# Layers' attention with the values stationary: two heads in two column halves, results that come out turned

## Chip, cores and metric

One core of one Trainium2 chip. The metric is the time of one execution in device microseconds (us), lower is better. TensorE is called PE here, its weight loads PEld, VectorE DVE, ScalarE ACT, GpSimd POOL, SyncE SP.

## What is computed

The reference is two blocks for one sequence of 256 tokens of width 1024, all in float32. The first block has attention, a gated delta rule and a routed mixture of 32 experts. The second block is two layers, and the change lies in their attention:

```python
for l in range(2):
    h = rms_norm(x, norm_mix[l]); z = h @ w_in[l]
    ...
    y_a = sparse_indexed_attention(qa, ka, va, qi, ki, wi, rel_bias, topk)   # 8 heads of 64
    y_b = latent_attention(qb, kb, vb)                                       # 8 heads, values of 64
    # each: p = softmax(logits); y = einsum('bthk,btkhd->bthd', p, v)
    gate_a = sigmoid(ga + b_gate[:D]); gate_b = sigmoid(gb + b_gate[D:])
    merged = gate_a * (y_a @ w_proj_a[l]) + gate_b * (y_b @ w_proj_b[l])
    x = x + merged @ w_out[l]
    ... # a gated convolutional feed-forward part
```

## The kernel before

Every engine has its own instruction list, and they meet through semaphores. Partition dimension is 128, so the 256 tokens are two token tiles (`tt` or `qt`, 0 and 1). PSUM is eight banks of 128 x 512 float32; `layer_plan` (L102) lists the jobs of a layer in the order in which banks are dealt out, round-robin over the eight. A producer waits for `room` (the bank's last user has read it), signals `full`; a reader waits for `ready`, signals `free`; `taken` is true once it has been read. So the order of names in that list decides which job waits for which. The layer's weights come in 2 MB pieces through four ring slots, loaded by SP; the load of a slot waits until the job that reads the slot's earlier weights is full (`loads2`, with the pair ("pa", 3) for the first projection).

The attention of a layer is four calls, `n` = 0 to 3: part a for token tile 0, part a for tile 1, part b for tile 0, part b for tile 1. A call for tile `qt` has `qt + 1` key tiles. Its steps:

- PE `scores` (L2048, through `scores_t`, L522; matmuls on L534) writes the scores of eight heads to `as` or `bs`. Heads are laid out by place: place p holds head 2(p % 4) + p // 4, that is 0, 2, 4, 6, 1, 3, 5, 7.
- DVE `soften_v` (L470) adds the bias or mask, takes the maximum.
- ACT `exps_s` (L507) writes the exponentials into `expo2[qt]` and their sums into `den[qt]`.
- PE `values_t` (L537) turns the exponentials, block by block of 128 x 128, into `at` or `bt` (L546), ACT `turned_s` (L516) copies each bank of four blocks to `PT2`, and PE multiplies (L554): a turned block (128 keys x 128 queries) is stationary, the head's values (128 keys x 64) move, so the result has the queries on its partitions and all eight heads side by side in one bank, `ao` or `bo`. An fp32 matmul is two instructions in the trace, a turn is one.
- DVE `result_v` (L497, its scaling on L502) divides by the sums and writes `ya` or `yb`, tokens on the partitions.
- PE `features("yaT")` turns `ya` (L576), ACT copies it, and `tokens("pa")` (matmuls on L604) multiplies it with the projection for both token tiles and two halves of 512 columns. The same for b.

PE's order behind the queries and keys is written out by hand (L2086 to L2103):

```python
scores(0) gates_t(1) scores(1) gates_t(2) values(0) scores(2) gates_t(3) values(1)
scores(3) values(2)  features yaT  tokens pa  values(3)  features ybT  tokens pb  turns mT  wo
```

DVE forms the gates (`gates_v`, a reciprocal of 128 x 1024 on L1771) between the calls, then multiplies the `pa` and `pb` banks with them (L1799, L1804) and adds (L1808) into `h`, whose storage is also `expo2[1]`. PE turns `h` (`mT`, L1988), ACT copies it, and `wo` follows (L604). Between the layers and ahead of the feed-forward part, `keep_running` (L581) issues twelve plain bf16 matmuls (L585) into the bank of the first `hT` or `fT`, for which it waits. `dn` are the four banks of the last projection of a layer, which DVE adds to `x` on L1630. The expert part uses half-width matmuls: 64 stationary columns, in column half 0 and column half 1 by turns (L1259, L1240).

Of the kernel before, what the change touches and what calls it, by code (L numbers as in the profile page):

```python
# [18 lines left out]
ALU = mybir.AluOpType  # L19
# [3 lines left out]
P = 128  # L23
T = 256
TT = T // P
D = 1024
# [75 lines left out]
def layer_plan():  # L102
    p = Plan()
    for name, n in (("hT", 4), ("cv", 1), ("qi", 2), ("m1", 2), ("m2", 2), ("kiT", 1), ("ix0", 2), ("ix1", 4),
# [4 lines left out]
                    ("wo", 4), ("fT", 4), ("up", 2 * UPC), ("dn", 4)):  # L109
        p.add(name, n)  # L110
    return p
# [106 lines left out]
def split(ap, n):  # L218
    return ap.rearrange("p (a b) -> p a b", a=n)
# [41 lines left out]
    "an_c", "an_q",  # L261
    "gsig",
    "b_in", "bst", "bn",
    "attn_m", "attn_e",
    "mg",
    "yconv", "fexp", "act",
    "out",
# [3 lines left out]
def build_program(nc, A, consts, out):  # L271
# [4 lines left out]
    with ctx:  # L276
# [45 lines left out]
        def area(at, n):  # L322
            return arena[:, at:at + n]
# [101 lines left out]
        def head(place):  # L425


            return 2 * (place % 4) + place // 4

        def ada_rows_t(pe, g):  # L430

            pe.wait_ge(*B.room(f"ag{g}"))
            rows = B.bank(f"ag{g}")
            for i in range(4):
                j = 4 * g + i
                pe.matmul(rows[32 * i:32 * i + 32, :], ident[0:12, j:j + 1].to_broadcast([12, 32]), badr[0:12, :],
                          start=True, stop=False)
            for a in range(4):
                w, landed = w1_slot(ada_at[g] + a)
                pe.wait_ge(*landed)  # L440
                for k in range(2):
                    for i in range(4):
                        ins = pe.matmul(rows[32 * i:32 * i + 32, :], silu_c[:, 2 * a + k, :],
                                        split(w, 2)[:, k, i * CH:(i + 1) * CH], start=False, stop=(a == 3 and k == 1))
            ins.then_inc(B.full(f"ag{g}"), 1)
# [51 lines left out]
        def result_v(v, then, B, S, jobs, call, dst, den, flag="attn_e"):  # L497
# [6 lines left out]
                            den.rearrange("p (b a) -> p b a", b=2).unsqueeze(3).to_broadcast([P, 2, 4, 64]), ALU.mult)\  # L504
             .then_inc(B.free(jobs[2]), 1)

        def exps_s(act, S, qt, call, scale, buf, amax, den):  # L507

            p4 = split(buf, 8)
            act.wait_ge(S["attn_m"], call + 1)  # L510
            for hd in range(8):
                ins = act.activation(p4[:, hd, :], p4[:, hd, :], ACT.Exp, bias=amax[:, hd:hd + 1], scale=scale,
                                     accum_out=den[:, hd:hd + 1])
            ins.then_inc(S["attn_e"], 1)
# [21 lines left out]

        def values_t(pe, B, S, jobs, qt, call, val, buf, PT, flag="attn_e"):  # L537

            p4 = split(buf, 8)
            pe.wait_ge(S[flag], call + 1)  # L540
            for j in range(2 * (qt + 1)):
                pe.wait_ge(*B.room(jobs[1], j))
                for i in range(4):
                    blk = 4 * j + i
                    hd, kt = blk // (qt + 1), blk % (qt + 1)
                    ins = pe.transpose(B.bank(jobs[1], j)[:, i * P:(i + 1) * P], p4[:, hd, kt * P:(kt + 1) * P], ident)  # L546
                ins.then_inc(B.full(jobs[1], j), 1)
            pe.wait_ge(*B.room(jobs[2]))
            for place in range(8):
                for kt in range(qt + 1):  # L550
                    blk = place * (qt + 1) + kt
                    if blk % 4 == 0:
                        pe.wait_ge(*B.taken(jobs[1], blk // 4))
                    ins = pe.matmul(B.bank(jobs[2])[:, place * 64:(place + 1) * 64], PT[:, blk * P:(blk + 1) * P],  # L554
                                    val(head(place), kt), start=(kt == 0), stop=(kt == qt))
            ins.then_inc(B.full(jobs[2]), 1)

        def mean_squares(act, count):

            for tt in range(TT):  # L560
                ins = act.activation(h[:, tt, :], x[:, tt, :], ACT.Square, accum_out=ss[:, tt:tt + 1])
            ins.then_inc(S["ss"], 1)
# [911 lines left out]
        qbT, kbT = split(extra(0, 2 * D), 8), split(extra(2 * D, 2 * D), 8)  # L1474
        qb, kb = split(extra(4 * D, 1536), TT), split(extra(4 * D + 1536, 1536), TT)
        vb = split(extra(4 * D + 3072, D), TT)
        ya, yb = split(area(4 * D, D), TT), split(area(5 * D, D), TT)
        yaT, ybT = split(area(9728, D), 4), split(area(10752, D), 4)
        expo2 = [area(8 * D, 8 * P), hbuf[:, 0:8 * T]]
        PT2 = extra(4 * D, 8 * T)  # L1480
# [168 lines left out]
        def layers_v(v):  # L1649
            for l in range(LAYERS):  # L1650
# [114 lines left out]
                def gates_v(i):  # L1765

                    for due in BL.all_taken((f"g{i}", 2)):
                        v.wait_ge(*due)
                    gs = gate_s[:, :, i * CH:(i + 1) * CH]
                    then(v.tensor_scalar(gs, gs, 1.0, None, ALU.add))  # L1770
                    v.reciprocal(gs, gs).then_inc(L["gsig"], 1)  # L1771

                def soften(nm, qt, n):
                    if nm == "a":
                        soften_v(v, then, BL, L, jobs2[nm][qt], qt, AHD ** -0.5, selm[qt], expo2[qt], amax[qt],
                                 bias=bias_t[qt])
                    else:
                        soften_v(v, then, BL, L, jobs2[nm][qt], qt, BQK ** -0.5, c(f"blkneg{qt}"), expo2[qt], amax[qt])


                v.wait_ge(S["rel_in"], 16 * 2 * TT)
                soften("a", 0, 0)
                gates_v(0)
                soften("a", 1, 1)
                gates_v(1)
                result_v(v, then, BL, L, jobs2["a"][0], 4 * l, ya[:, 0, :], den[0])
                soften("b", 0, 2)
                gates_v(2)
                result_v(v, then, BL, L, jobs2["a"][1], 4 * l + 1, ya[:, 1, :], den[1])
                soften("b", 1, 3)  # L1790
                result_v(v, then, BL, L, jobs2["b"][0], 4 * l + 2, yb[:, 0, :], den[0])
                gates_v(3)

                v.wait_ge(L["gsig"], 4 * l + 4)
                for j in range(4):
# [1 line left out]
                    g = gate_s[:, tt, half * CH:(half + 1) * CH]  # L1797
                    v.wait_ge(*BL.ready("pa", j))
                    v.tensor_tensor(g, BL.bank("pa", j)[:], g, ALU.mult).then_inc(BL.free("pa", j), 1)  # L1799
                result_v(v, then, BL, L, jobs2["b"][1], 4 * l + 3, yb[:, 1, :], den[1])  # L1800
                for j in range(4):
                    tt, half = j // 2, j % 2
                    v.wait_ge(*BL.ready("pb", j))
                    v.tensor_tensor(mtmp[j % 2], BL.bank("pb", j)[:], gate_s[:, tt, D + half * CH:D + (half + 1) * CH], ALU.mult)\  # L1804
                     .then_inc(BL.free("pb", j), 1)
                    v.wait_ge(*BL.taken("pb", j))
                    v.wait_ge(*BL.taken("pa", j))
                    v.tensor_tensor(h[:, tt, half * CH:(half + 1) * CH], gate_s[:, tt, half * CH:(half + 1) * CH],  # L1808
                                    mtmp[j % 2], ALU.add).then_inc(L["mg"], 1)
                norm_v(v, BL, "wo", 2 * l + 1, normw[0])  # L1810
# [27 lines left out]
        def layers_s(act):  # L1838
            for l in range(LAYERS):
# [84 lines left out]
                gates_s(1)  # L1924
                exps(1)
                gates_s(2)
                turned_s(act, BL, jobs2["a"][0], 0, PT2)
                exps(2)
                gates_s(3)
                turned_s(act, BL, jobs2["a"][1], 1, PT2)  # L1930
                turned_s(act, BL, jobs2["b"][0], 0, PT2)
                copy("yaT", 2, pair(yaT))
                exps(3)
                turned_s(act, BL, jobs2["b"][1], 1, PT2)
                copy("ybT", 2, pair(ybT))
                copy("mT", 4, pair(mT))
                squares("wo")
                copy("fT", 4, pair(hT))
# [16 lines left out]
        def layers_t(pe):  # L1955
            for l in range(LAYERS):
# [100 lines left out]

                def values(n):
                    val = va if n < 2 else vb
                    values_t(pe, BL, L, jobs2["ab"[n // 2]][n % 2], n % 2, 4 * l + n,  # L2060
                             lambda hd, kt: val[:, kt, hd * 64:(hd + 1) * 64], expo2[n % 2], PT2)

                tokens("aq", weights(), KT)
                tokens("ak", weights(), KT)
# [28 lines left out]
                values(1)  # L2093
                scores(3)
                values(2)
                wait_taken("ao1", 1)
                features("yaT", ya, 4)
                tokens("pa", weights(), 4, src=yaT, widths=(CH, CH), turned="yaT")
                values(3)
                wait_taken("bo1", 1)  # L2100
                features("ybT", yb, 4)
                tokens("pb", weights(), 4, src=ybT, widths=(CH, CH), turned="ybT")
                features_by_tile("mT", h, lambda tt, half: (L["mg"], 4 * l + 2 * tt + half + 1))  # L2103
                ws = [weights(), weights()]
                for tt in range(TT):
# [389 lines left out]
```

## Time and profile before

| | |
|---|---|
| median of 3 runs | 2282.95 us (2274.84, 2282.95, 2283.5) |
| the profiled execution | 2281.05 us, span 2279.2 us |
| mean granted PE clock | 0.986 |
| busy: PE, PEld, DVE, ACT, POOL | 2168.5, 1123.0, 872.5, 331.1, 49.2 us |
| HBM | 601.36 MB read, 265 GB/s over the span |

The span holds the first block with its experts up to about 1300 us, then the two layers. The page's slices show PE busy in almost every one; DMA is busy for 9 tenths in the expert part and for about 1 to 7 tenths in the layers. In the views in order of time, a line's second number is the time from the first start to the last end of the group, and ends overlap the next group's start; the difference of two starts is what a group costs its engine. The number in brackets is idle time ahead of the group, with what ended it.

### The profile page before, as it was taken

To read this page: it belongs to the slowest core of one execution; us is meant where nothing else is said; L and a number is where in the kernel's file an instruction comes from. 1 tells how busy PE (TensorE), PEld (TensorE's weight loads), DVE (VectorE), ACT (ScalarE), POOL (GpSimd) and SP (SyncE) were. 2 spreads that over 40 slices of the span, in tenths; PEclk is the share of its full clock that TensorE was granted. 3 is DMA by queue.
4 is the path that set the end of the run, shared out by engine and by line. 5 is a ranking of instruction groups with operands and counts; after the bars stand their busy time and mean duration, and the time that the engine had idled before them with its cause. 6 is when DMAs were issued, how large, how long until landed. Compare 5 with 4: busy or idle time off the path is not lost.

```text
span 2279.2 us, 22906 instructions
## 1 busy us (share of the span) xinstructions
PE 2168.5 (95%) x9380; PEld 1123.0 (49%) x9385; DVE 872.5 (38%) x1332; ACT 331.1 (15%) x720; POOL 49.2 (2%) x30
## 2 busy tenths in 40 slices
PE   6998889999999999999999999999999999999999
PEld 4856643333333333333333365557884555658874
DVE  0555343333222233333332235643661166525640
ACT  1133110000000000000000112221210112311110
POOL 0000100000000000000000002000000011000000
PEclk9988989999999999999999999999999999999999
DMA  9555049999999999999999744234442534244441
GB/s 372 205 225 230 1 147 403 427 429 428 428 429 428 429 428 429 428 428 428 429 429 429 310 169 167 104 118 141 155 148 92 182 127 163 78 144 130 162 152 37
DMA packets 132825, 603.35 MB, mean 265 GB/s; under 512 B 9222, under 2 KB 65686, under 8 KB 104090
## 3 DMA queue, kind: packets, MB, share of 16 engines
q1 hardware_dynamic: 132762, 602.45, 66.5%
q8 instruction: 47, 0.77, 0.1%
q14 instruction: 16, 0.13, 0.0%
HBM read 601.36 MB, written 3.16 MB: 265 GB/s over the span
## 4 chain that ended last, share of the span: by engine, by line
PE 64%; DMA 29%; DVE 3%; ACT 1%; issue 1%; POOL 0%; SPq 0%; POOLq 0%; DVEq 0%
DMA ring<-in_w_dram 28%; PE bank L594 18%; PE bank L604 12%; PE bank L1259 11%; PE bank L2123 7%; PE bank L2044 5%; PE bank L803 2%; PE bank L2416 1%; PE bank L554 1%; DMA ring<-in_w_ada_dram 1%; PE bank L534 1%; PE bank L1240 1%; PE bank L1306 1%; PE bank L576 0%; PE bank L546 0%
## 5 line engine op out<-in xcount | busy, mean ns | idle before, releaser
L1259 PE MATMUL bank<-ring,arena 128*64 128x512 f32 x3168 | 707.1, 597 | 38.4 <-DMA ring<-in_w_dram 37.0
L1259 PEld LDWEIGHTS bank<-ring,arena 128*64 128x64 f32 x3168 | 218.0, 137 | 518.7 <-issue 416.9
L594 PE MATMUL bank<-hTbuf,ring 128*128 128x256 f32 x1856 | 403.7, 380 | 2.8 <-ACT hTbuf L2305 2.6
L594 PEld LDWEIGHTS bank<-hTbuf,ring 128*128 128x128 f32 x1856 | 353.5, 191 | 52.5 <-issue 4.3
L1012 DVE TENSOR_SCALAR arena<-bank 128x512 f32<-128x512 f32 x33 | 22.8, 691 | 431.4 <-PE bank L1259 431.4
L2123 PE MATMUL bank<-ring 128*128 128x512 f32 x352 | 151.4, 592 | 0.0
L604 PE MATMUL bank<-ring,hTbuf 128*128 128x512 f32 (+2 forms) x384 | 151.2, 554 | 0.0
L1820 DVE SCALAR_TENSOR_TENSOR arena<-bank,arena 128x254 f32<-128x254 f32 (+1 forms) x176 | 76.6, 477 | 119.0 <-ACT arena L1947 117.4
L2044 PE MATMUL bank<-ring,hTbuf 128*128 128x512 f32 x256 | 112.0, 596 | 0.0
L1016 DVE RECIPROCAL arena<-arena 128x512 f32<-128x512 f32 x33 | 110.6, 3353 | 1.1
L604 PEld LDWEIGHTS bank<-ring,hTbuf 128*128 128x128 f32 x384 | 72.7, 190 | 75.1 <-issue 71.8
L2123 PEld LDWEIGHTS bank<-ring 128*128 128x128 f32 x352 | 66.9, 190 | 83.3 <-issue 83.2
L1120 ACT ACTIVATE arena<-arena 128x512 f32<-128x512 f32 x33 | 20.8, 629 | 561.2 <-DVE arena L1012 561.2
L604 PE MATMUL bank<-ring,arena 128*128 128x512 f32 (+1 forms) x208 | 85.8, 569 | 1.4 <-ACT arena L1855 1.4
L2044 PEld LDWEIGHTS bank<-ring,hTbuf 128*128 128x128 f32 x256 | 48.0, 190 | 63.4 <-issue 63.4
L1630 DVE TENSOR_TENSOR x<-x,bank 128x512 f32<-128x512 f32 x16 | 11.0, 687 | 172.5 <-PE bank L2123 126.3
L1947 ACT ACTIVATE arena<-bank,arena 128x256 f32<-128x256 f32 x88 | 44.9, 560 | 209.5 <-PE bank L594 209.5
L1832 DVE RECIPROCAL arena<-arena 128x512 f32<-128x512 f32 x22 | 73.8, 3353 | 0.8
L1306 PE MATMUL bank<-arena 64*128 64x512 f32 x264 | 65.6, 615 | 8.0 <-DVE arena L1036 8.0
L1036 DVE TENSOR_TENSOR arena<-bank,arena 128x512 f32<-128x512 f32 x33 | 22.8, 691 | 128.2 <-PE bank L1259 128.2
L1240 PE MATMUL bank<-hbuf,arena 128*64 128x512 f32 x264 | 65.6, 619 | 1.9 <-DVE arena L1005 1.9
L604 PEld LDWEIGHTS bank<-ring,arena 128*128 128x128 f32 x208 | 39.1, 190 | 44.8 <-issue 44.3
(369 smaller groups left out, 1716.7 us busy)
## 6 DMA issues: line engine op xcount, KB each, us to landing
ring<-in_w_dram SPq DMA_DIRECT2D x198, 2048.0 KB, 24.2
ring<-in_w_up_dram SPq DMA_DIRECT2D x44, 1024.0 KB, 7.4
ring<-in_w_in_dram SPq DMA_DIRECT2D x21, 2048.0 KB, 7.7
ring<-in_w_ada_dram SPq DMA_DIRECT2D x12, 2048.0 KB, 8.9
ring<-in_w_down_dram SPq DMA_DIRECT2D x10, 2048.0 KB, 7.7
ring<-in_w_out_dram SPq DMA_DIRECT2D x6, 2048.0 KB, 9.0
ring<-in_w_in_dram SPq DMA_DIRECT2D x4, 1024.0 KB, 13.5
ring<-in_w_proj_a_dram SPq DMA_DIRECT2D x2, 2048.0 KB, 7.8
```

Of the source, the lines that this page charges most:

```text
L594: ins = pe.matmul(B.bank(name, j)[:, i * T:(i + 1) * T], w[:, k, (first + i) * P:(first + i + 1) * P], hT[:, k, :], start=(k == 0), stop=( ...
L604: ins = pe.matmul(B.bank(name, j)[:, 0:width], xs(k), ws(k), start=(k == 0), stop=(k == kts - 1))
L803: return lambda out, u: pe.matmul(out, lhsT[:, u, :], rhs[:, u, :], start=True, stop=True)
L1016: v.reciprocal(eb, eb).then_inc(F["s1"], 1)
L1240: ins = pe.matmul(XB[g * SLOTS:(g + 1) * SLOTS, :], psel[:, tt, :], h[:, tt, g * CH:(g + 1) * CH], start=(tt == 0), stop=(tt == 1))
L1259: ins = pe.matmul(bank[g * SLOTS:(g + 1) * SLOTS, :], lhsT, rhs[:, g * CH:(g + 1) * CH], start=start, stop=stop)
L1306: pe.matmul(ACC[2 * tt + g][:], pgt[par][64 * g:64 * g + 64, tt, :], ysb[64 * g:64 * g + 64, :], start=False, stop=False, skip_group_check ...
L1820: ins = v.scalar_tensor_tensor(out=y2[:, k, back:], in0=pb[:, k, 0:T - back], scalar=conv_cols[:, 44 * (2 - back) + m:44 * (2 - back) + m ...
L1832: then(v.reciprocal(fe[i % 2], fe[i % 2]))
L1947: ins = act.activation(split(y, 2)[:, k, :], pb[:, k, :], ACT.Identity, scale=conv_cols[:, 88 + m:89 + m], bias=conv_cols[:, 132 + m:133 + m])
L2044: ins = pe.matmul(BL.bank(f"g{i}", tt)[:], hT[:, k, tt * P:(tt + 1) * P], w[:, k, :], start=False, stop=(k == KT - 1))
L2123: ins = pe.matmul(BL.bank("dn", 2 * tt + half)[:], actT[:, k, tt * P:(tt + 1) * P], w_of[k][:, k % 4, half * CH:(half + 1) * CH], start=(k ...
```

## The change

The values become the stationary operand. For each pair of heads and each key tile, PE loads the head's values (128 keys x 64) and moves the turned probabilities (128 keys x 128 queries); the even head writes partitions 0 to 63 of the bank, the odd head 64 to 127. The result has head features on the partitions and tokens along the row, so it needs no turn and is copied by ACT (`heads_s`) straight into `yaT` or `ybT`. The division by the sums moves ahead of the turn: DVE `shares_v` takes the reciprocals and multiplies the whole tile of exponentials, and PE's turn waits for `attn_p` instead of `attn_e`. The jobs `yaT` and `ybT` leave the bank plan and `pb` moves ahead of `bt1`. The projection is issued by token tile: `pa` for both, `pb` for tile 0, then `values(3)`, then `pb` for tile 1. DVE waits for `ao0` and `ao1` before it overwrites the exponentials, and for the last bank of `bt1` before it writes `h`.

```diff
-                    ("bo0", 1), ("yaT", 2), ("pa", 4), ("bt1", 4), ("bo1", 1), ("ybT", 2), ("pb", 4), ("mT", 4),
+                    ("bo0", 1), ("pa", 4), ("pb", 4), ("bt1", 4), ("bo1", 1), ("mT", 4),
...
+        def place_of(hd):
+            return hd // 2 + 4 * (hd % 2)
...
+        def shares_v(v, then, S, qt, call, buf, den):
+            p4 = split(buf, 8)
+            v.wait_ge(S["attn_e"], call + 1)
+            then(v.reciprocal(den, den))
+            v.tensor_tensor(p4, p4, den.unsqueeze(2).to_broadcast([P, 8, P * (qt + 1)]), ALU.mult).then_inc(S["attn_p"], 1)
+            v.wait_ge(S["attn_p"], call + 1)
...
                 soften("a", 0, 0)
                 gates_v(0)
+                shares(0)
                 soften("a", 1, 1)
                 gates_v(1)
-                result_v(v, then, BL, L, jobs2["a"][0], 4 * l, ya[:, 0, :], den[0])
+                shares(1)
+                v.wait_ge(*BL.ready("ao0"))
                 soften("b", 0, 2)
                 gates_v(2)
-                result_v(v, then, BL, L, jobs2["a"][1], 4 * l + 1, ya[:, 1, :], den[1])
+                shares(2)
+                v.wait_ge(*BL.ready("ao1"))
                 soften("b", 1, 3)
-                result_v(v, then, BL, L, jobs2["b"][0], 4 * l + 2, yb[:, 0, :], den[0])
                 gates_v(3)
+                shares(3)
...
-                result_v(v, then, BL, L, jobs2["b"][1], 4 * l + 3, yb[:, 1, :], den[1])
                 for j in range(4):
...
+                    if j == 0:
+                        v.wait_ge(*BL.ready("bt1", 3))
                     v.tensor_tensor(h[:, tt, half * CH:(half + 1) * CH], gate_s[:, tt, half * CH:(half + 1) * CH],
...
+                def heads_s(name, dst, qt):
+                    act.wait_ge(*BL.ready(name))
+                    act.activation(dst[:, :, qt * P:(qt + 1) * P], split(BL.bank(name)[:], 4), ACT.Copy)\
+                       .then_inc(BL.free(name), 1)
...
                 turned_s(act, BL, jobs2["a"][0], 0, PT2)
+                heads_s("ao0", yaT, 0)
                 exps(2)
                 gates_s(3)
                 turned_s(act, BL, jobs2["a"][1], 1, PT2)
+                heads_s("ao1", yaT, 1)
                 turned_s(act, BL, jobs2["b"][0], 0, PT2)
-                copy("yaT", 2, pair(yaT))
+                heads_s("bo0", ybT, 0)
                 exps(3)
                 turned_s(act, BL, jobs2["b"][1], 1, PT2)
-                copy("ybT", 2, pair(ybT))
+                heads_s("bo1", ybT, 1)
...
+                    turn_t(pe, BL, L, jobs, qt, 4 * l + n, expo2[qt], "attn_p")
+                    pe.wait_ge(*BL.room(jobs[2]))
+                    seen = set()
+                    for two in range(4):
+                        for kt in range(qt + 1):
+                            for g in range(2):
+                                blk = place_of(2 * two + g) * (qt + 1) + kt
+                                if blk // 4 not in seen:
+                                    seen.add(blk // 4)
+                                    pe.wait_ge(*BL.taken(jobs[1], blk // 4))
+                                hd = 2 * two + g
+                                ins = pe.matmul(BL.bank(jobs[2])[64 * g:64 * g + 64, two * P:(two + 1) * P],
+                                                val[:, kt, hd * 64:(hd + 1) * 64], PT2[:, blk * P:(blk + 1) * P],
+                                                start=(kt == 0), stop=(kt == qt))
...
-                wait_taken("ao1", 1)
-                features("yaT", ya, 4)
-                tokens("pa", weights(), 4, src=yaT, widths=(CH, CH), turned="yaT")
+                project_t("pa", weights(), yaT, "ao", (0, 1))
+                wpb = weights()
+                project_t("pb", wpb, ybT, "bo", (0,))
                 values(3)
-                wait_taken("bo1", 1)
-                features("ybT", yb, 4)
-                tokens("pb", weights(), 4, src=ybT, widths=(CH, CH), turned="ybT")
+                project_t("pb", wpb, ybT, "bo", (1,))
```

`turn_t` is the first half of `values_t`, unchanged; `project_t` waits per token tile until `ao` or `bo` of that tile has been copied and then calls `token_major` for its two column halves. The first block's attention is not changed.

## Rows read from the trace of the kernel before

**Rows 1.** The page, busy time of PE: us, share of the span, instructions.
```profile
PE 2168.5 (95%) x9380; PEld 1123.0 (49%) x9385; DVE 872.5 (38%) x1332; ACT 331.1 (15%) x720; POOL 49.2 (2%) x30
```
**Rows 2.** Busy time by stretch: us, PE, PEld, DVE, ACT, POOL, clock, DMA share, GB/s.
```profile
1457.72:1528.63 70.91, 68.44 (x310) 42.79 (x308) 33.55 (x33) 18.02 (x53) 0.00 (x0) 1.00 0.32 107
1944.71:2015.62 70.91, 68.44 (x309) 42.79 (x308) 33.56 (x33) 18.02 (x53) 0.00 (x0) 1.00 0.27 91
```
**Rows 3.** PE in order of time, attention of the first layer: start, us, what.
```profile
1457.72 1.04 PE L546 MATMUL bank<-con,arena 128*128 128x128 f32 x8
1459.15 1.97 PE L554 MATMUL bank<-arena,ring 128*128 128x64 f32 x16 [0.39 <-ACT ring L520]
1460.95 2.00 PE L534 MATMUL bank<-ring 96*128 96x128 f32 x16
...
1479.53 3.68 PE L554 MATMUL bank<-arena,ring 128*128 128x64 f32 x32
1483.05 3.67 PE L534 MATMUL bank<-ring 96*128 96x256 f32 x16
...
1489.74 1.04 PE L576 MATMUL bank<-con,arena 128*128 128x128 f32 x8
1491.13 13.97 PE L604 MATMUL bank<-ring,arena 128*128 128x512 f32 x32 [0.34 <-ACT arena L1855]
...
1506.68 3.68 PE L554 MATMUL bank<-ring 128*128 128x64 f32 x32
1511.22 1.09 PE L576 MATMUL bank<-con,arena 128*128 128x128 f32 x8 [0.85 <-DVE arena L502]
1512.65 13.97 PE L604 MATMUL bank<-ring,arena 128*128 128x512 f32 x32 [0.34 <-ACT arena L1855]
1526.46 1.47 PE L1988 MATMUL bank<-con,hbuf 128*128 128x128 f32 x12
```
**Rows 4.** ACT in order of time, same stretch.
```profile
1457.92 0.60 ACT L1892 ACTIVATE arena<-bank 128x512 f32<-128x512 f32 x1 [4.57 <-PE bank L2044]
1458.41 1.08 ACT L520 ACTIVATE ring<-bank 128x512 f32<-128x512 f32 x2
...
1478.47 2.06 ACT L520 ACTIVATE ring<-bank 128x512 f32<-128x512 f32 x4
```
**Rows 5.** DVE in order of time, attention of the first layer.
```profile
1425.95 1.23 DVE L485 TENSOR_TENSOR arena<-arena 128x1024 f32<-128x1024 f32 x1
...
1443.98 2.29 DVE L485 TENSOR_TENSOR hbuf<-hbuf,arena 128x2048 f32<-128x2048 f32 x1
...
1491.54 6.55 DVE L1771 RECIPROCAL arena<-arena 128x1024 f32<-128x1024 f32 x1
...
1510.47 0.69 DVE L502 TENSOR_TENSOR arena<-bank,small 128x512 f32<-128x512 f32 x1 [4.54 <-PE bank L554]
...
1526.66 0.69 DVE L1804 TENSOR_TENSOR arena<-bank,arena 128x512 f32<-128x512 f32 x1 [2.02 <-PE bank L604]
```
**Rows 6.** PE in order of time, in the expert part.
```profile
708.70 3.65 PE L1259 MATMUL bank<-ring,arena 128*64 128x512 f32 x16 [1.24 <-DMA ring<-in_w_dram]
712.28 0.66 PE L1289 MATMUL bank<-con,arena 128*128 128x128 f32 x4
...
725.23 1.09 PE L1271 MATMUL bank<-arena 32*64 32x512 f32 x8
726.25 9.30 PE L1259 MATMUL bank<-ring,arena 128*64 128x512 f32 x42
```
**Rows 7.** Weight loads by line and shape: busy us, mean ns of one; idle before.
```profile
L1259 PEld LDWEIGHTS bank<-ring,arena 128*64 128x64 f32 x3168 | 218.0, 137 | 518.7 <-issue 416.9 <-DMA ring<-in_w_dram 99.8 <-ACT arena L1124 1.9
...
L554 PEld LDWEIGHTS bank<-arena,ring 128*128 128x128 f32 x96 | 11.0, 192 | 1.2 <-issue 1.2
```
**Rows 8.** PE and DVE in order of time, between the two layers.
```profile
1789.12 2.54 PE L585 MATMUL bank<-con 128*128 128x512 bf16 x11
1792.92 1.09 PE L1988 MATMUL bank<-con,hbuf 128*128 128x128 f32 x8 [0.39 <-DVE hbuf L1642]
...
1789.10 0.69 DVE L1630 TENSOR_TENSOR x<-x,bank 128x512 f32<-128x512 f32 x1 [0.17 <-PE bank L2123]
```

More of the change, by code:

```diff
@@ L263 @@
     "b_in", "bst", "bn",
-    "attn_m", "attn_e",
+    "attn_m", "attn_e", "attn_p",
     "mg",
@@ L537, in values_t, with turn_t @@
         def values_t(pe, B, S, jobs, qt, call, val, buf, PT, flag="attn_e"):
+            turn_t(pe, B, S, jobs, qt, call, buf, flag)
+            pe.wait_ge(*B.room(jobs[2]))
+            for place in range(8):
+                for kt in range(qt + 1):
+                    blk = place * (qt + 1) + kt
+                    if blk % 4 == 0:
+                        pe.wait_ge(*B.taken(jobs[1], blk // 4))
+                    ins = pe.matmul(B.bank(jobs[2])[:, place * 64:(place + 1) * 64], PT[:, blk * P:(blk + 1) * P],
+                                    val(head(place), kt), start=(kt == 0), stop=(kt == qt))
+            ins.then_inc(B.full(jobs[2]), 1)
+        def turn_t(pe, B, S, jobs, qt, call, buf, flag):
             p4 = split(buf, 8)
@@ L547, in values_t @@
                 ins.then_inc(B.full(jobs[1], j), 1)
[L548 to L556, printed above, removed]
         def mean_squares(act, count):
@@ L1476, in build_program @@
         vb = split(extra(4 * D + 3072, D), TT)
-        ya, yb = split(area(4 * D, D), TT), split(area(5 * D, D), TT)
         yaT, ybT = split(area(9728, D), 4), split(area(10752, D), 4)
@@ L1781, in layers_v, with shares @@
                 v.wait_ge(S["rel_in"], 16 * 2 * TT)
+                def shares(n):
+                    shares_v(v, then, L, n % 2, 4 * l + n, expo2[n % 2], den[n % 2])
                 soften("a", 0, 0)
                 gates_v(0)
+                shares(0)
                 soften("a", 1, 1)
                 gates_v(1)
-                result_v(v, then, BL, L, jobs2["a"][0], 4 * l, ya[:, 0, :], den[0])
+                shares(1)
+                v.wait_ge(*BL.ready("ao0"))
                 soften("b", 0, 2)
                 gates_v(2)
-                result_v(v, then, BL, L, jobs2["a"][1], 4 * l + 1, ya[:, 1, :], den[1])
+                shares(2)
+                v.wait_ge(*BL.ready("ao1"))
                 soften("b", 1, 3)
-                result_v(v, then, BL, L, jobs2["b"][0], 4 * l + 2, yb[:, 0, :], den[0])
                 gates_v(3)
+                shares(3)
                 v.wait_ge(L["gsig"], 4 * l + 4)
@@ L2059, in values @@
                     val = va if n < 2 else vb
-                    values_t(pe, BL, L, jobs2["ab"[n // 2]][n % 2], n % 2, 4 * l + n,
-                             lambda hd, kt: val[:, kt, hd * 64:(hd + 1) * 64], expo2[n % 2], PT2)
+                    qt, jobs = n % 2, jobs2["ab"[n // 2]][n % 2]
+                    turn_t(pe, BL, L, jobs, qt, 4 * l + n, expo2[qt], "attn_p")
+                    pe.wait_ge(*BL.room(jobs[2]))
+                    seen = set()
+                    for two in range(4):
+                        for kt in range(qt + 1):
+                            for g in range(2):
[7 more added lines that the diff above has]
+                                                start=(kt == 0), stop=(kt == qt))
+                    ins.then_inc(BL.full(jobs[2]), 1)
                 tokens("aq", weights(), KT)
@@ L2095, in layers_t, with project_t @@
                 values(2)
-                wait_taken("ao1", 1)
-                features("yaT", ya, 4)
-                tokens("pa", weights(), 4, src=yaT, widths=(CH, CH), turned="yaT")
+                def project_t(name, w, src, heads, tiles):
+                    for tt in tiles:
+                        pe.wait_ge(*BL.taken(f"{heads}{tt}"))
+                        for half in range(2):
+                            token_major(pe, BL, name, 2 * tt + half, lambda k: src[:, k, tt * P:(tt + 1) * P],
+                                        lambda k: w[:, k, half * CH:(half + 1) * CH], 4)
+                project_t("pa", weights(), yaT, "ao", (0, 1))
+                wpb = weights()
+                project_t("pb", wpb, ybT, "bo", (0,))
                 values(3)
-                wait_taken("bo1", 1)
-                features("ybT", yb, 4)
-                tokens("pb", weights(), 4, src=ybT, widths=(CH, CH), turned="ybT")
+                project_t("pb", wpb, ybT, "bo", (1,))
                 features_by_tile("mT", h, lambda tt, half: (L["mg"], 4 * l + 2 * tt + half + 1))
```

## Prediction, made before the result was known

> **What bounds the kernel now.** I read first the busy shares of the page: the matmul engine is busy for 95% of the span [rows 1]. Most of the span is the expert part, which the change does not touch; the change lies in the two layers behind it. So the second view is the table by stretch for the attention of each layer, from the first turn of probabilities (`values(0)`) to the first matmul of `wo`. Each stretch takes 70.91 us in both layers, PE is busy for 68.44 of it at a granted clock of 1.00, DVE for 33.6, ACT for 18.0, and the transfers take about a third of the DMA engines [rows 2]. PE is the bound, and it has no large wait: what counts is what PE issues and the few gaps between. The third view is PE in order of time [rows 3]. Its starts give the pace of each piece, since the start of the next piece is where an instruction stops costing PE anything (the printed times overlap). A short matmul costs PE 0.11 us whatever it moves: 16 value instructions with 64 moving columns take 1.80 us (1459.15 to 1460.95), 32 take 3.52.
>
> **What the change does to PE, per layer.** Times are those of the first layer; the second has the same pattern.
>
> *The turns of the results go.* `features("yaT")` takes from 1489.74 to 1491.13: 1.39 us for eight turns and the wait for their copy. Nothing takes its place, because `ao0` and `ao1` were copied long before. `features("ybT")` with its wait for DVE's scaling of `bo1` takes from 1510.20 (1506.68 plus 3.52) to 1512.65, 2.45 us [rows 3]. In its place PE waits for ACT to copy `bo1` ahead of token tile 1 of `pb`: 0.27 until the bank is full (DVE's L502 starts at 1510.47), 0.60 for an ACT copy of a bank, and 0.14 from a copy's end to the matmul behind it (1459.01 to 1459.15), 1.01 together [rows 3 to 5]. Gain 1.44. ACT's new copy writes four pieces of 128 columns; I take the time of the plain one.
>
> *The values.* The instruction count stays (16 and 32), each now moves 128 columns through 64 stationary ones, and consecutive heads go to the two column halves. Do the halves run side by side? The expert part shows that they do: 16 instructions of 128x64 with 512 moving columns take 3.58 us, 0.22 each, where a full-width one of the same length takes 0.43 (32 in 13.8 us, 1512.65 to 1526.46) [rows 3, 6]. So 128 columns should cost about 0.108 us a pair, and I take 0.112, the pace that short ones hold today. Weight loads need not stand in the way: a 64-column load is shown at 137 ns against 192 [rows 7], and 192 is hidden today at 0.112. What is worse than before is the start: the first pair is head 0 and head 1, whose blocks lie half the places apart, so its second half waits for the second copied bank of two, or the third of four. For a first tile the second copy ends at 1459.49 (1458.41 plus 1.08), so that half starts at 1459.63; eight steps of 0.112 later it is 1460.53. In the expert part 16 such instructions take 3.58 where eight pairs at 0.43 are 3.44: 0.14 for entering and leaving the half-width form [rows 6]. Entering lies here under the wait for the first copy; for leaving I take 0.10 (bounds 0 and 0.14). That gives 1460.63 against 1460.95, a gain of 0.32. For a second tile the copies step by 0.487 (2.06 less 0.60, by three), the third ends at 1480.04, its matmul starts at 1480.18, 16 steps end at 1481.97, with the exit 1482.07 against 1483.05: gain 0.98 [rows 3, 4]. Two of each per layer are 2.60, and `values(3)` has its exit under a wait anyway: 2.70.
>
> The Trainium skill (TensorEngine Tiling, Performance Considerations) speaks against part of this: each matmul has an overhead of about 60 cycles, and one should not tile along a dimension that is already small. By that rule the sum would be smaller, by how much rival 2 works out from rows; at 512 columns the trace shows two halves at the cost of one full-width instruction, and no run here shows short ones.
>
> *The end of the merge.* The banks are dealt anew. `mT` now takes the banks of `pb` 1, 2, 3 and `bt1` 0, where it had banks free long before. So the third pair of turns of tile 0 waits until DVE has read `pb` 3: 0.90 after PE's last `pb` issue (1526.46 to 1527.36, [rows 5]) instead of nothing, after only four turns, and twelve follow. `mT` 0 is then full at about 1528.23, its copy (0.05 and 0.60) lets `wo` start at 1529.0 instead of 1528.63. Loss 0.37. Bounds: 0 and, if the next copy too came late, 0.9.
>
> Per layer 2.70 + 1.39 + 1.44 - 0.37 = 5.16; both 10.32.
>
> *Between the layers* `hT` 0 now lies on the bank of `dn` 3. The warming matmuls of the second layer start at about 1789.0 today (twelve are issued, the record of the first is missing), as `hT` 0's bank is free; they will wait until DVE has read `dn` 3 (1789.10 plus 0.69). That is 0.80 later, of which the wait of 0.39 ahead of the second tile's turns takes up a part [rows 8]: cost about 0.36 to 0.4, taken as 0.36, bounds 0 and 0.8. The first layer and the last are not touched by it.
>
> **What other engines get.** DVE loses four scalings of 0.69 per layer and gets four of whole probability tiles. L485, the same operation on the same sizes, took 1.23 us for 1024 columns and 2.29 for 2048 [rows 5]. That is 7.0 for 2.8, on an engine with 37 us free in the stretch. They delay nothing if they come before PE asks. The tightest is `shares(3)`: it stands behind the gate reciprocal (1491.54 plus 6.55) and ends at about 1500.6; PE asks for it after `pa` and the first half of `pb`, about 1508.9. Eight us of cover; `shares(0)` to `(2)` have over ten. Behind `shares(3)` stand the `pa` products, whose banks `bt1` needs at 1508.9: four of 0.69 after 1500.6, also in time, as PE fills the last `pa` bank only near 1502. The new wait of DVE on `bt1` 3 ahead of its first write to `h` holds the read of `pb` 1 until about 1511, and PE needs that bank only for `mT`. ACT loses four turned copies and gets four, none where `exps` are late. SP's queue is not moved past anything: `pa` 3 is ready earlier, so the `up` loads start no later, with two thirds of DMA idle.
>
> **The sum:** 10.32 - 0.36 = 10.0 us less. The profiled execution took 2281.05 (span 2279.2), giving 2271.1; the median of the runs shown is 2282.95, 1.9 above, and I put the forecast there: **2273 us**. The forecast's own range, with the bounds of its small terms, is 8.4 to 11.7 less.
>
> **Rivals.**
> 1. *The halves do not pair at 128 columns*: every instruction costs 0.112. Once the second copy is there 14 or 30 of them remain, 88 per layer. Per layer the values then take 88 x 0.112 + 2.26 (the late starts) = 12.1 against 10.64, and with the other terms the run gains 2 x (10.64 + 2.46 - 12.1) - 0.36 = 1.6: 2281.3. For it: both passes of an fp32 matmul go to the same half one after the other. Against: that is so in the expert part too, and it pairs.
> 2. *An overhead per instruction that shows when several parts of the array run at once.* The quarter-size rows of the expert part hint at one: 8 instructions on 32 rows and 64 columns take 1.02 us (725.23 to 726.25), 0.128 each, where four at once should take 0.43 / 4 = 0.107 [rows 6]. With that 0.021 on each 0.054 a first tile takes 0.48 + 1.20 + 0.10 = 1.78, a second 0.65 + 2.40 + 0.10 = 3.15; the values gain 0.88 per layer and the run 2 x (0.88 + 2.46) - 0.36 = 6.3: 2276.6. The overhead that the Trainium skill's page on tiling states is a thing of this kind. Against: 0.22 per long half-width instruction leaves no room for it.
> 3. *Slower: the loads of the halves come into the open.* If each 137 ns load [rows 7] stands ahead of its 0.112 us of moving, an instruction costs 0.249; the same formula gives 2 x (88 x 0.249 + 2.26 - 13.1) + 0.36 = 22.5 us more, 2305. It decides from 0.121 us per instruction (no gain) and is clearly slower from 0.186. For it: loads of both halves fall into 0.11 us, which no row of before has. Against: full-width loads of 192 ns are hidden at that pace.
> 4. *The gain is larger*: the pairs leave without an exit price, `mT` and `hT` cost nothing: 11.7 less, 2271.3.
>
> **How the numbers follow.** Forecast 0.68, rival 1 0.09, rival 2 0.11, rival 3 0.05, rival 4 0.07. About 0.5%, 11.4 us, is what a measurement of this kernel can tell from no change. The forecast lies 1.4 us short of that bound; runs of before alone span 2274.84 to 2283.5, so even with the sum right the measured change may come out on the other side: of the forecast's 0.68 I give 0.30 to faster, of rival 4 0.05, of rival 2 0.01. Slower gets rival 3. The range goes from 2266, the larger gain with the spread of runs, to 2281, which reaches nearly to rival 1.
>
> **What would show it.** In PE's order of time: 16 value instructions in about 1.4 us and 32 in about 2.4 with starts in pairs (right), 1.8 or more (rivals 1, 3); no turns on L576 in the layer's attention behind `qaT` and `kaT`; one gap of about 0.9 us behind `values(3)`, ended by ACT; a gap of about 0.5 ended by DVE inside the turns of `mT`; the stretch from `values(0)` to `wo` near 65.8 us instead of 70.91. A wait of PE on DVE's products ahead of `values` would prove the cover wrong; a stretch of 65.8 us with an unchanged run would mean that the time went elsewhere, which nothing here lets me expect.

## The result and the profile after

| | before | after |
|---|---|---|
| median of 13 runs each | 2283.16 us (2274.84 to 2286.03) | 2271.24 us (2267.15 to 2273.61) |
| profiled execution, span | 2281.05, 2279.2 us | 2267.62, 2265.6 us |

The ratio is 0.9947 with a 95% interval of 0.9937 to 0.9957: 0.53% faster, 11.9 us by the medians. The forecast was 2273. Each ratio leaves out disturbed executions, here and below: one of the kernel before (2330.76 us) and one of turned_in_pairs (4537.66 us). The change of the profiled executions is 13.4 us, that of the medians 11.9, and the forecast had 10.0. To see which of these is the change's own, the first view is PE in order of time where the layers begin: the first turn of the first layer's `h`, once in the kernel before and once in the one after.

```profile
1304.82 2.20 PE L1988 MATMUL bank<-con,hbuf 128*128 128x128 f32 x16
```

```profile
1301.59 2.20 PE L2016 MATMUL bank<-con,hbuf 128*128 128x128 f32 x16
```

From there to the end of the span it is 974.38 us before (2279.2 - 1304.82) and 964.01 after (2265.6 - 1301.59): 10.37 us less. The other 3.2 us of the profiled pair come ahead of the layers, in code that the change does not touch. The experiments below say what to make of them.

Next the table by stretch for the same piece as in [rows 2], from `values(0)` to the first matmul of `wo`, in both layers of the kernel after.

```profile
1454.49:1519.96 65.47, 63.53 (x293) 36.18 (x292) 34.81 (x31) 18.24 (x53) 0.00 (x0) 1.00 0.36 119
1936.46:2001.92 65.46, 63.52 (x293) 36.17 (x292) 34.80 (x31) 18.24 (x53) 0.00 (x0) 1.00 0.31 101
```

70.91 us have become 65.47. PE is busy 4.9 us less, with 17 and 16 recorded instructions fewer (the sixteen turns that are gone; some records are missing), and its idle time falls from 2.47 to 1.94 us. DVE is busy only 1.3 us more in this stretch, because `shares(0)` and most of `shares(1)` lie ahead of it: of the seven us of multiplications 4.34 fall into the first layer's stretch, and 2.77 of scalings went. Then PE in order of time, the rows that answer to [rows 3].

```profile
1454.49 1.04 PE L571 MATMUL bank<-con,arena 128*128 128x128 f32 x8
1455.92 1.49 PE L2100 MATMUL bank<-ring,arena 128*64 128x128 f32 x16 [0.39 <-ACT ring L532]
1457.33 2.05 PE L546 MATMUL bank<-ring 96*128 96x128 f32 x16
...
1474.21 1.91 PE L571 MATMUL bank<-con,hbuf 128*128 128x128 f32 x16
1476.05 2.44 PE L2100 MATMUL bank<-ring,arena 128*64 128x128 f32 x32
1478.42 3.72 PE L546 MATMUL bank<-ring 96*128 96x256 f32 x16
...
1483.36 1.48 PE L2100 MATMUL bank<-ring 128*64 128x128 f32 x16 [0.34 <-ACT ring L532]
1484.77 20.87 PE L619 MATMUL bank<-ring,arena 128*128 128x512 f32 x48
1505.47 1.91 PE L571 MATMUL bank<-con,hbuf 128*128 128x128 f32 x16
1507.32 2.39 PE L2100 MATMUL bank<-ring 128*64 128x128 f32 x32
1510.39 7.13 PE L619 MATMUL bank<-ring,arena 128*128 128x512 f32 x16 [0.69 <-ACT arena L1950]
1517.36 0.60 PE L2016 MATMUL bank<-con,hbuf 128*128 128x128 f32 x4
1518.31 1.53 PE L2016 MATMUL bank<-con,hbuf 128*128 128x128 f32 x12 [0.35 <-DVE arena L1823]
1519.96 27.70 PE L619 MATMUL bank<-ring 128*128 128x512 f32 x64
```

Read the starts. The 16 value instructions of a first tile take 1.41 us (1455.92 to 1457.33) where they took 1.80, the 32 of a second tile 2.37 where they took 3.52. Behind `values(2)` the projection starts at once. Behind `values(3)` there is one wait, ended by ACT's copy of `bo1` (L1950). In the turns of `mT` there is the new wait on DVE's read of `pb` 3 (L1823), after four turns.

Next DVE in order of time: `shares(3)` (L516 with 2048 columns) with the gate's reciprocal ahead of it and the products of `pa` behind it.

```profile
1486.13 6.55 DVE L1785 RECIPROCAL arena<-arena 128x1024 f32<-128x1024 f32 x1
1492.60 0.14 DVE L515 RECIPROCAL small<-small 128x8 f32<-128x8 f32 x1
1492.78 2.29 DVE L516 TENSOR_TENSOR hbuf<-hbuf,small 128x2048 f32<-128x2048 f32 x1
1495.11 1.89 DVE L1819 TENSOR_TENSOR arena<-bank,arena 128x512 f32<-128x512 f32 x3
```

It is done at 1495.07, and PE asks for it at 1505.47: ten us of cover. Last the one line of ACT that ends the wait for `bo1`, its copy:

```profile
1509.74 0.60 ACT L1950 ACTIVATE arena<-bank 128x512 f32<-128x512 f32 x1 [1.56 <-PE bank L2100]
```

### The profile page after: what moved, and what is told of

Read it like the earlier page. It is cut to its first block, busy times and chain, and to the rows that moved or that the text cites. A ratio compares the mean times of both kernels' runs of the same rounds, so it can differ in the third digit from the quotient of the medians.

```text
span 2265.6 us, 22840 instructions
## 1 busy us (share of the span) xinstructions
PE 2155.1 (95%) x9348; PEld 1106.4 (49%) x9353; DVE 880.8 (39%) x1332; ACT 332.1 (15%) x720; POOL 49.2 (2%) x30
## 4 chain that ended last, share of the span: by engine, by line
PE 64%; DMA 29%; DVE 3%; ACT 1%; issue 1%; SPq 0%; POOL 0%; POOLq 0%; DVEq 0%
DMA ring<-in_w_dram 28%; PE bank L609 18%; PE bank L619 12%; PE bank L1274 11%; PE bank L2171 7%; PE bank L2072 5%; PE bank L818 2%; PE bank L2464 1%; DMA ring<-in_w_ada_dram 1%; PE bank L546 1%; PE bank L1255 1%; PE bank L1321 1%; PE bank L2100 1%; PE bank L600 0%; PE bank L2016 0%
```

## The experiments

Each kernel is an edit of the kernel after, and ran beside the kernel before. Since the part ahead of the layers moves by itself, the sharper measure is the one used above: from the first turn of the first layer to the end of the span, in the kernel's own profiled execution. It is called "in the layers" here. The end of a span is printed to 0.1 us, so these numbers are good to 0.05. Some expectations start at the warming matmuls instead; by that measure the changed kernel takes the 967.85 us that they name, and differences are the same but for 0.2 where the record of the first is missing.

| kernel | layers start | in the layers | against after | median of the runs, ratio to before (95%) |
|---|---|---|---|---|
| before | 1304.82 | 974.38 | +10.37 | |
| after | 1301.59 | 964.01 | 0 | 2271.24, 0.9947 (0.9937 to 0.9957) |
| after_again | 1299.20 | 964.00 | 0 | 2272.22, 0.9960 (0.9944 to 0.9975) |
| after_third | 1307.07 | 964.03 | 0 | 2270.89, 0.9944 (0.9931 to 0.9957) |
| halves_apart | 1305.38 | 967.92 | +3.91 | 2276.83, 0.9971 (0.9959 to 0.9984) |
| turned_in_pairs | 1308.10 | 960.70 | -3.31 | 2268.88, 0.9943 (0.9923 to 0.9962) |
| b_behind | 1308.06 | 961.54 | -2.47 | 2268.26, 0.9942 (0.9922 to 0.9962) |
| warm_bank | 1307.31 | 963.69 | -0.32 | 2272.47, 0.9954 (0.9939 to 0.9970) |
| no_division | 1305.24 | 964.06 | +0.05 | 2271.93, 0.9951 (0.9935 to 0.9966) |
| all_three | 1301.55 | 957.85 | -6.16 | 2266.40, 0.9929 (0.9916 to 0.9943) |
| all_three_again | 1305.56 | 957.84 | -6.17 | 2263.18, 0.9914 (0.9900 to 0.9929) |

The medians of after_again, halves_apart, turned_in_pairs and b_behind come from one chip, those of warm_bank, no_division and all_three from a second, those of all_three_again and after_third from a third. A median is best compared inside its group.

**The changed kernel again** (after_again, and after_third on another chip; no edit).

> The changed kernel once more, beside the variants of it. If the sum of the prediction is the whole effect (about 10.4 us in the layers of the profiled execution), the median lies 9 to 12 us under the kernel before. If the 13.4 us between the two profiled executions were all due to the change, 12.5 to 14 us. The part ahead of the layers is the same work in both, so the start of the layers should move by some us from execution to execution for either kernel; if it is always 3 us earlier in the changed kernel, something there is due to the change after all.

> The changed kernel for the third time. The layers should take 967.8 us again, from the first warming matmul with a record to the last matmul; the ratio to the kernel before 0.9950 to 0.9960 if only the 10.4 us of the layers count, 0.9940 if 13.4 us do.

In the layers the three executions agree within 0.03 us, while the layers start anywhere from 1299.20 to 1307.07. Over all eleven traces the start runs from 1299.2 to 1308.1, and the kernel before, at 1304.8, lies in the middle. So the 3.2 us of the first profiled pair lie within the spread of the part ahead, and the change's own effect is 10.4 us, 0.45%. The three ratios fit as well: their differences to 1 are 0.40, 0.53 and 0.56%, and each interval holds 0.9955. The first expectation gave 9 to 12 us under the kernel before, and it was 9.7. The second gave 0.9950 to 0.9960 for 10.4 us and 0.9940 for 13.4; 0.9944 lies outside the first, nearer to the second, and its interval (0.9931 to 0.9957) holds values of both. So the ratios alone hardly decide between the two readings; the starts of the layers do. What makes the part ahead take longer or shorter was not pursued.

**Do the halves run side by side?** halves_apart issues all even heads, then all odd heads.

```diff
-                    for two in range(4):
-                        for kt in range(qt + 1):
-                            for g in range(2):
+                    for g in range(2):
+                        for two in range(4):
+                            for kt in range(qt + 1):
```

> All even heads first (column half 0), then all odd heads (half 1), so no two neighbours lie in different halves; nothing else changes. Theory (the gain on the values comes from two halves running side by side): 16 value instructions take 1.6 to 1.8 us instead of 1.41, 32 take 3.3 to 3.5 instead of 2.37, starts 0.11 apart but for an overlap at the one change of half; the run is 4 to 6 us slower than the changed kernel, 2275 to 2277. Rival (64-column loads and the longer moving operand alone make it cheap, order does not matter): values stay at 1.41 and 2.37, the run at 2271.

PE in order of time, halves_apart, first layer:

```profile
1459.71 1.55 PE L2100 MATMUL bank<-ring,arena 128*64 128x128 f32 x16 [0.39 <-ACT ring L532]
1461.19 2.05 PE L546 MATMUL bank<-ring 96*128 96x128 f32 x16
...
1479.91 3.33 PE L2100 MATMUL bank<-ring,arena 128*64 128x128 f32 x32
1483.16 3.72 PE L546 MATMUL bank<-ring 96*128 96x256 f32 x16
```

The same instructions with the same loads now take 1.48 and 3.25 us instead of 1.41 and 2.37. For a second tile that is 0.102 us an instruction against 0.074, with the late start of the paired order still in the 2.37. Order alone costs 3.91 us (4.6 by the medians of the same chip), so the rival that order does not matter has fallen. Both times are below the expected 1.6 to 1.8 and 3.3 to 3.5, and the loss in the layers just below 4 to 6 us: 16 serial steps of 0.109 would be 1.74. About a quarter of a microsecond was saved in both lengths, and the starts of the single instructions in the trace show where. In the second tile they come one at a time, 0.109 apart, up to 1481.27; then eight starts come in 0.38 us (1481.27, 1481.27, 1481.38, 1481.43, 1481.49, 1481.54, 1481.60, 1481.65), and behind them one at a time again. The first tile has the same stretch from 1460.17 on. A record does not name its half. But these are two interleaved rows of starts 0.109 apart (the first step of the second row is 0.16), and 1481.27 is the thirteenth start of sixteen in the first half, so the first three instructions of the second half ran beside the last three of the first. In a first tile this order has another merit, no late start, which is why it loses only 0.07 us there.

**What does the late start cost?** turned_in_pairs turns the blocks in the order in which the pairs want them.

```diff
+                    if paired:
+                        hd, kt = blk // 2 // (qt + 1) + 4 * (blk % 2), blk // 2 % (qt + 1)
...
-                                blk = place_of(2 * two + g) * (qt + 1) + kt
+                                blk = 2 * (two * (qt + 1) + kt) + g
```

> Only the order in which the blocks are turned changes: the two heads of a pair stand side by side in the copied banks, so the first pair needs the first bank alone. Theory (the late start is what is left of the cost): the idle time inside the values goes; from the first turn to the end of the values 2.4 us instead of 2.84 for a first tile, 3.4 instead of 4.21 for a second, bounded by copies 0.49 apart; 2.0 to 2.5 us per layer, the run 4 to 5 us faster than the changed kernel, 2266 to 2267. Rival (PE is held by the rate of the pairs, not by the start): under 1 us.

PE in order of time, turned_in_pairs, first layer:

```profile
1460.99 1.04 PE L573 MATMUL bank<-con,arena 128*128 128x128 f32 x8
1462.42 1.09 PE L2102 MATMUL bank<-ring,arena 128*64 128x128 f32 x16 [0.39 <-ACT ring L532]
1463.45 2.05 PE L546 MATMUL bank<-ring 96*128 96x128 f32 x16
...
1480.32 1.91 PE L573 MATMUL bank<-con,hbuf 128*128 128x128 f32 x16
1482.16 1.97 PE L2102 MATMUL bank<-ring,arena 128*64 128x128 f32 x32
1484.06 3.72 PE L546 MATMUL bank<-ring 96*128 96x256 f32 x16
```

Without a wait inside them 16 instructions take 1.03 us and 32 take 1.90: the 16 more cost 0.87, which is 0.109 a pair, and 0.16 stays. The single starts say what it is made of: in each half the first instruction takes 0.13 to 0.16 to the next start instead of 0.109, and 0.20 pass from the last start to the next piece. Where no wait stands ahead of the values, 0.09 more is paid before them, as the turns then take 1.84 instead of 1.75. From the first turn to the end of the values it is 2.46 (expected 2.4) for a first tile and 3.74 for a second, where I expected 3.4. The size was wrong there: I let the last copied bank set the end, but 16 pairs at 0.109 take longer than the copies, and they cannot start before the turns end. The gain is 3.31 us in the layers, not 4 to 5. By the medians of the same chip it is 3.3 us (2272.22 to 2268.88), though the intervals of the two ratios overlap; the expected 2266 to 2267 was missed.

**What does splitting part b's projection cost?** b_behind lets `values(3)` come first and both token tiles follow.

```diff
-                    ("bo0", 1), ("pa", 4), ("pb", 4), ("bt1", 4), ("bo1", 1), ("mT", 4),
+                    ("bo0", 1), ("pa", 4), ("bt1", 4), ("bo1", 1), ("pb", 4), ("mT", 4),
...
-                project_t("pb", wpb, ybT, "bo", (0,))
                 values(3)
-                project_t("pb", wpb, ybT, "bo", (1,))
+                project_t("pb", wpb, ybT, "bo", (0, 1))
```

> The projection of part b goes wholly behind values(3), with its banks dealt behind bo1, as before the change; by token tile it stays. Theory: the wait for the copy of bo1 (0.69 us) hides behind token tile 0, and the banks of mT are free long before, so the wait of 0.35 in its turns goes back to 0.2; values(3) is asked for at about 1498.6 in the first layer, 3.5 us after shares(3) is done. 1.0 to 1.3 us per layer, the run 2 to 2.6 us faster than the changed kernel. Rival (the split was needed as cover for shares(3)): PE waits for DVE ahead of values(3), gain under 0.5 us or a loss.

PE in order of time, b_behind, first layer:

```profile
1491.24 14.00 PE L619 MATMUL bank<-ring,arena 128*128 128x512 f32 x32
1505.08 1.91 PE L571 MATMUL bank<-con,hbuf 128*128 128x128 f32 x16
1506.92 2.39 PE L2100 MATMUL bank<-ring 128*64 128x128 f32 x32
1509.24 14.00 PE L619 MATMUL bank<-ring,arena 128*128 128x512 f32 x32
1523.07 1.47 PE L2016 MATMUL bank<-con,hbuf 128*128 128x128 f32 x12
1524.75 0.66 PE L2016 MATMUL bank<-con,hbuf 128*128 128x128 f32 x4 [0.20 <-DVE hbuf L1829]
1525.24 27.63 PE L619 MATMUL bank<-ring 128*128 128x512 f32 x64
```

There is no wait ahead of `values(3)` and none for `bo1`; the turns of `mT` take 2.17 us as before the change, and `wo` 27.69 instead of 27.76. 2.47 us in the layers, as expected (4.0 by the medians of the same chip, more than the layers account for). So of the change's own edits this one, the split with its order of banks, costs time: tile 0 of part b would have covered the copy better behind `values(3)` than ahead of it.

**The bank of the warming matmuls.** warm_bank issues them into the bank of `hT` 1.

```diff
-                    pe.wait_ge(*BL.room("hT", 0))
-                    keep_running(pe, BL.bank("hT", 0), 12)
+                    pe.wait_ge(*BL.room("hT", 1))
+                    keep_running(pe, BL.bank("hT", 1), 12)
```

> Only the bank of the twelve warming matmuls between the layers changes (hT 1 instead of hT 0). Theory: the gap of 1.01 us ahead of them goes and a wait of about 0.4 for the second tile comes back, so the layers take 0.4 to 0.6 us less than 967.85, which the run's time cannot show. Rival (they start late for another reason, DVE's norm): nothing, 967.8.

PE in order of time between the layers, first the kernel after, then warm_bank:

```profile
1781.48 2.54 PE L600 MATMUL bank<-con 128*128 128x512 bf16 x11 [1.01 <-DVE x L1644]
1783.85 1.91 PE L2016 MATMUL bank<-con,hbuf 128*128 128x128 f32 x16
```

```profile
1786.02 2.75 PE L600 MATMUL bank<-con 128*128 128x512 bf16 x12
1788.61 1.04 PE L2016 MATMUL bank<-con,hbuf 128*128 128x128 f32 x8
1790.04 1.09 PE L2016 MATMUL bank<-con,hbuf 128*128 128x128 f32 x8 [0.39 <-DVE hbuf L1656]
```

The idle 1.01 us (0.2 of it a missing record) goes, and a wait of 0.39 ahead of the second tile comes back. 0.32 us, near the forecast's 0.36 and a little below the expected 0.4 to 0.6.

**Is the division really beside the path?** no_division leaves the multiplication of the layers' probabilities by their reciprocal sums out.

```diff
-            v.tensor_tensor(p4, p4, den.unsqueeze(2).to_broadcast([P, 8, P * (qt + 1)]), ALU.mult).then_inc(S["attn_p"], 1)
+            v.tensor_copy(den, den).then_inc(S["attn_p"], 1)
```

> The layers' probabilities are not divided by their sums: the multiplication of the whole tile on DVE is left out, a copy of eight columns signals in its place. Theory (the four multiplications, 7 us of DVE per layer, lie wholly beside PE): the layers take 967.85 us, within 0.1. Rival (DVE's work is partly on the path, by a product of pa or pb that comes late): 0.3 us per layer or more is gained.

964.06 us against 964.01. Seven us of DVE work per layer cost nothing.

**All three together.** The edits of turned_in_pairs, b_behind and warm_bank in one kernel, twice.

> Blocks turned in the order of the pairs, part b's projection wholly behind values(3), and the warming matmuls of the second layer in the bank of hT 1, which is free early. From the first warming matmul of the first layer to the last matmul the changed kernel takes 967.85 us in both its traces; turned_in_pairs took 3.3 less and b_behind 2.5 less by the same measure. Theory (three separate gaps of PE, each on the path): they add up, with 0.4 to 0.5 for the warming: 6.1 to 6.4 less, 961.5 in the layers, the run at 2264 to 2266. Rival (taking one gap away opens a wait for DVE, above all for shares(3) with 3 us of cover): less than 5 us.

> The version with all three edits again, on one chip with the changed kernel. In the layers its trace took 6.2 us less than the changed kernel's. If that is the whole difference, its median lies 4 to 8 us under the changed kernel's in the same call. If the part ahead of the layers reacts to the layers' code, the medians differ by something else.

PE in order of time, all_three, from `values(2)` on:

```profile
1482.45 1.09 PE L2102 MATMUL bank<-ring 128*64 128x128 f32 x16 [0.34 <-ACT ring L532]
1483.48 14.00 PE L621 MATMUL bank<-ring,arena 128*128 128x512 f32 x32
1497.32 1.91 PE L573 MATMUL bank<-con,hbuf 128*128 128x128 f32 x16
1499.15 1.97 PE L2102 MATMUL bank<-ring 128*64 128x128 f32 x32
1501.05 14.00 PE L621 MATMUL bank<-ring,arena 128*128 128x512 f32 x32
```

The parts are 3.31, 2.47 and 0.32, 6.10 in sum; together they give 6.16 and 6.17. The gaps add up, and no new wait opens: `shares(3)` still ends 3 us ahead of the turns at 1497.32 (DVE, 1491.88 plus 2.29). The rival, under 5 us, is out. The first ratio is 0.9929 (its median of 2266.40 lies just above the expected 2264 to 2266), the second 0.9914. On the third chip the median lies 7.7 us under the changed kernel's, where 4 to 8 were expected, and their intervals do not overlap. This version beats both kernels: 16.5 us in the layers against the kernel before.

## Why the prediction was right

The range, 2266 to 2281, holds the measured 2271.24, and the sum of 10.0 us stands against 10.37 in the layers. By its own steps, per layer in us:

| step | forecast | measured | from |
|---|---|---|---|
| values of part a, first tile | 0.32 | 0.39 | 3.23 to 2.84, first turn to next work |
| values of part a, second tile | 0.98 | 1.06 | 5.27 to 4.21 |
| first tile of b and the turns of `ya` | 1.71 | 1.78 | 4.57 to 2.79 |
| second tile of b and the turns of `yb` | 2.52 | 2.79 | 7.71 to 4.92 |
| turns of `mT` | -0.37 | -0.43 | 2.17 to 2.60 |
| first matmul behind the half-width form, and other | 0 | -0.15 | scores and projection 0.05 longer each |
| sum | 5.16 | 5.44 | 70.91 to 65.47 |
| between the layers, once | -0.36 | about -0.34 | from `wo` to the second `values(0)` it is 0.42 longer, 0.08 of it in `wo`; warm_bank gives 0.32 |
| `wo`, twice | 0 | -0.15 | 27.68 to 27.76 in each layer; gone in b_behind |

**The pairing** was the step on which most hung, and it was taken from the expert part's 512-column rows. halves_apart shows it: order alone is worth 3.91 us. The gain is 0.07 to 0.08 larger per call than forecast, and the single starts show which term that was. The second half starts 0.05 us behind the end of the copy it needs (1476.53 behind 1476.47), not the 0.14 that I had read at the first copy; counted from the first turn that is 2.32 instead of 2.40. The other two errors cancel: a pair step is 0.109, not 0.112, which is 0.05 less over sixteen steps, and entering and leaving take 0.15 from there on, not 0.10. Entering also makes the turns ahead 0.09 longer in a second tile (1474.21 to 1476.05 is 1.84, it was 1.75). That costs nothing, because the second half waits for its copy in any case.

**The wait for `bo1`** was taken as 1.01. The second half of `values(3)` starts at 1507.74, so its sixteen steps end at 1509.49, ACT's copy starts at 1509.74 and takes 0.60, and the projection starts at 1510.39: 0.90, with 0.05 behind the copy's end where 0.14 was taken. These 0.11, the earlier start of the second half (2.27 behind the first turn, not 2.40) and the faster pairs make up the 0.27, which is the largest difference of the table.

**The late start** was right as a mechanism, and turned_in_pairs took 3.31 us of it away. **The new wait in `mT`** came where the bank plan put it, with 0.43 for 0.37. **DVE's cover** was larger than said: `shares(3)` ended 10 us ahead, not 8. Counted from `values(0)`, the gate's reciprocal ahead of it starts 2.2 us earlier than before, as the scores of the fourth call come 1.4 us earlier and the scalings ahead of it are gone; the forecast had left it where it was. And no_division shows that it costs nothing.

**The rivals.** No pairing at all (2281.3) and exposed loads (2305) are out: 0.109 a pair. An overhead per instruction that shows only with several parts at work (2276.6) is out too: it wanted 0.15 a pair. The row that hinted at it holds the same price once per group and not per instruction: its eight start four at a time, at 725.23 and 725.71, and the next piece starts at 726.25, two steps of 0.43 with 0.05 and 0.10 more, 0.16 together. At half width 128 columns cost 0.109 us a pair, a quarter of the 0.43 that 512 columns take, so nothing is added per instruction. The Trainium skill (TensorEngine Tiling, Performance Considerations) states an overhead of about 60 cycles for each matmul, and that one with a free dimension of 1 takes as long as one of 60. As an addition the trace does not show it; whether it holds as a floor for shorter ones no run here shows. The larger gain did not come as it was thought (no exit price, no loss at `mT` and `hT`), since the exit and both bank waits were there; that the medians differ by 11.9 us, near its 11.7, is the spread of the part ahead.

**The chances.** I gave 0.59 to a change within 0.5% and 0.36 to more. The layers' own effect is 0.45%, on the side where most of the chance lay; the first measurement came out at 0.53%, the second at 0.40, the third at 0.56. That is what a forecast 1.4 us short of the bound can expect of runs that spread over more than that: on which side one measurement falls is luck.

## What to carry to other kernels

Where each head has few value columns, make the values stationary and give neighbouring instructions to different column halves; it pays by their order, so write the order out, and turn the blocks in the order in which the pairs want them. A result that comes out with its features on the partitions saves a turn and a copy, as long as the division can move to an engine with time to spare. When jobs leave or move in a round-robin bank plan, go through every later `room` as well: two of the four losses here were banks that had become somebody else's.

## What the runs showed of the hardware that was not expected

A short pair of half-width instructions has hardly any price of its own: 0.109 us for two of 128 columns, with 0.16 once for entering and leaving and 0.09 more ahead of it where no wait hides that (1.84 us of turns instead of 1.75). And the halves overlapped a little even when issued one after the other: 16 instructions with a single change of half took 1.48 us where serial steps would take 1.74, because the first three of the second half ran beside the last three of the first.
